# Start of a decoder step: the order of the first loads, dummy products, mixed chunks, and row factors spread without diagonals

## The reference, cut to what matters

```python
def rmsnorm(x, g):
    y = xf * lax.rsqrt(jnp.mean(xf * xf, -1, keepdims=True) + EPS)
    return (y * g).astype(x.dtype)

u = rmsnorm(x, norm_mix) @ w_in        # x: 520 x 1024, w_in: 1024 x 1216
cq, ckv, kr, up = u[..., :384], u[..., 384:640], u[..., 640:704], u[..., 704:]
c = rmsnorm(ckv, kv_norm)
...                                    # attention, pooling, memory attention, SwiGLU, final norm
```

## Time and profile before

| | us |
|---|---|
| median of 3 runs | 798.16 |
| lowest and highest | 796.25, 798.38 |
| span of the profiled execution | 797.1 |
| TensorE busy | 760.2 |
| DVE busy | 593.8 |
| ACT busy | 395.1 |
| GpSimd busy | 125.3 |

### The profile page before, as it was taken

The page is one execution under the profiler, slowest core; times in us unless marked ns, Lnnn a source line. Parts: engine busy times, 40 slices in busy tenths (PEclk is TensorE's granted clock), DMA queues, the critical chain, the costliest instruction groups (busy, mean ns, idle before and its releaser), DMA issues. The chain is left out here.

```text
span 797.1 us, 16215 instructions
## 1 busy us (share of the span) xinstructions
PE 760.2 (95%) x6264; PEld 727.7 (91%) x6264; DVE 593.8 (75%) x1170; ACT 395.1 (50%) x850; POOL 125.3 (16%) x179
## 2 busy tenths in 40 slices
PE   6999998897999997899999999999999999999996
PEld 6999887874899997888899999999999999999996
DVE  5778674687467699666478899888888869876664
ACT  5523776422265333665344356555555558433344
POOL 0376303230004731000046000000000000000000
PEclk9999999999999999999999999999999999999999
DMA  9423333462597558895243214333333333334303
GB/s 269 114 54 87 102 107 145 146 214 104 169 307 239 180 171 254 276 360 175 79 122 107 74 42 122 109 103 104 104 102 105 106 90 108 111 106 121 103 16 108
DMA packets 141777, 109.96 MB, mean 138 GB/s; under 512 B 9733, under 2 KB 133726, under 8 KB 138621
## 3 DMA queue, kind: packets, MB, share of 16 engines
q1 hardware_dynamic: 134830, 90.65, 37.5%
q0 software_dynamic: 3104, 14.68, 5.6%
q10 hardware_dynamic: 3767, 3.59, 1.3%
HBM read 103.93 MB, written 5.20 MB: 137 GB/s over the span
## 5 line engine op out<-in xcount | busy, mean ns | idle before, releaser
L1968 DVE TENSOR_TENSOR wlo<-wraw,whi 128x512 fp32r<-128x512 f32 (+1 forms) x178 | 129.8, 765 | 44.5 <-ACT whi L1271 34.7
L2906 PE MATMUL ps<-B_hi,whi 128*128 128x260 f32 x384 | 110.6, 288 | 2.4 <-DVE B_lo L1969 1.2
L2908 PE MATMUL ps<-B_hi,wlo 128*128 128x260 f32 x384 | 108.9, 284 | 0.0
L2907 PE MATMUL ps<-B_lo,whi 128*128 128x260 f32 x384 | 108.9, 283 | 0.0
L1271 ACT ACTIVATE whi<-wraw 128x512 fp32r<-128x512 f32 (+1 forms) x138 | 78.6, 616 | 53.9 <-DMA wraw<-in_w_mv_dram 10.7
L2906 PE MATMUL ps<-A_hi,whi 128*128 128x260 f32 x264 | 76.6, 290 | 0.3 <-ACT kn_lo L1365 0.3
L2906 PEld LDWEIGHTS ps<-B_hi,whi 128*128 128x128 f32 x384 | 72.8, 190 | 3.3 <-issue 1.5
L2907 PE MATMUL ps<-A_lo,whi 128*128 128x260 f32 x264 | 75.2, 285 | 0.0
L2908 PE MATMUL ps<-A_hi,wlo 128*128 128x260 f32 x264 | 75.1, 284 | 0.0
L2907 PEld LDWEIGHTS ps<-B_lo,whi 128*128 128x128 f32 x384 | 72.9, 190 | 0.0
L2908 PEld LDWEIGHTS ps<-B_hi,wlo 128*128 128x128 f32 x384 | 72.8, 190 | 0.0
(11 more groups left out here) (560 smaller groups left out, 2388.9 us busy)
## 6 DMA issues: line engine op xcount, KB each, us to landing
kv_slot<-in_cache_mem_k_dram SPq DMA_DIRECT2D x8, 1024.0 KB, 8.9
kv_slot<-in_cache_mem_v_dram SPq DMA_DIRECT2D x8, 1024.0 KB, 8.1
wraw<-in_w_out_dram SPq DMA_DIRECT2D x14, 512.0 KB, 4.3
wraw<-in_w_up_dram SPq DMA_DIRECT2D x12, 512.0 KB, 4.4
xraw<-in_w_gate_dram SPq DMA_DIRECT2D x20, 256.0 KB, 3.6
xraw<-in_w_up_dram SPq DMA_DIRECT2D x10, 512.0 KB, 4.1
wraw<-in_w_in_dram SPq DMA_DIRECT2D x9, 512.0 KB, 4.2
wraw<-in_w_gate_dram SPq DMA_DIRECT2D x18, 256.0 KB, 4.3
```

The lines of the kernel that those rows point to most:

```text
L1968: return dve.tensor_tensor(dst, src, high.bitcast(F32), ALU.subtract)
L2906: pe.matmul(dst, left[0], right[0], start=first, stop=False)
L2907: pe.matmul(dst, left[0], right[1], start=False, stop=False)
L2908: return pe.matmul(dst, left[1], right[0], start=False, stop=last)
```

## The change

- SyncE: tile 0 of w_in is issued ahead of x, and x comes in four quarters (256 columns, a semaphore each), then tile 1.
- TensorE: one dummy product (all-ones matrices, 512 columns, f32, into `accO`) before the identity is awaited, two more after the samples are turned.
- TensorE: chunks 0 and 1 are turned when the first quarter is in, 2 and 3 with the second, and so on. Chunks 0 and 1 of tile 0, turn 4 and 5, chunks 2 and 3 of tile 0, turn 6 and 7, chunks 0 to 3 of tile 1, then chunks 4 to 7 of both tiles in turn.
- ACT and DVE: both parts of an even chunk are read from PSUM; DVE's copy comes after its low part. ACT's copy and high part of odd chunks are as before. The samples' square comes first on ACT, ahead of the split of tile 0; row 1 is squared by DVE instead of ACT; the split of tile 2 is moved ahead of the last step of the row factors on both engines.
- Row factors, at both places: no diagonals; TensorE takes a column of factors, repeated 128 times, as loaded operand and the identity as the other.

```diff
-    o += [("in", 0, f) for f in (0, 1)] + [("xt", 6), ("xt", 7), ("bc",)] + [("in", 1, f) for f in (0, 1)]
+    o += [("in", 0, f) for f in (0, 1)] + [("xt", 6), ("xt", 7)] + [("in", 1, f) for f in (0, 1)] + [("bc",)]
...
-            for i in (0, 1):
-                half = slice(i * 512, (i + 1) * 512)
-                sp.dma_start(x_nat[:, 0:4, half], a["x_prompt"][0].rearrange("(t p) d -> p t d", p=P)[:, :, half]).then_inc(x_in[i], 16)
-                load_w(i)
+            load_w(0)
+            for i in range(4):
+                part = slice(i * 256, (i + 1) * 256)
+                sp.dma_start(x_nat[:, 0:4, part], a["x_prompt"][0].rearrange("(t p) d -> p t d", p=P)[:, :, part]).then_inc(x_in[i], 16)
+            load_w(1)
...
+            act.wait_ge(xs_in, 16)
+            act.activation(x_sq[0:NB, 3, :], x_nat[0:NB, 4, :], ACT.Square, accum_out=n1[0:NB, 4:5]).then_inc(x_squared, 1)
+            split_w(0)
             for c in range(KD):
...
-                    after(("x1", c))
-                    high(("x1", c), B_hi[:, c, 0:TP], xT[:, c, 0:TP], gain(G_MIX + c))
-                if c == 0:
-                    split_w(0)
+                    high(("x1", c), B_hi[:, c, 0:TP], full(act, ("xt", c)), gain(G_MIX + c))
                 if c == 3:
                     split_w(1)
+                if c == 5:
                     row_square(0)
-                if c == 5:
-                    row_square(1)
             row_square(3)
...
+            split_w(2)
             after(("ms", "n1"))
...
+                src = xT[:, c, 0:TP] if c % 2 else full(dve, ("xt", c))
+                low(("x1", c), B_lo[:, c, 0:TP], src, B_hi[:, c, 0:TP], gain(G_MIX + c))
...
             split_w(0)
+            for c in range(KD):
+                low_x(c)
+                if c % 2 == 0:
+                    copy_x(c)
+                if c == 3:
+                    split_w(1)
...
+            row_square(1, x_sq[:, 1, :])
+            row_square(2, x_sq2[:, :])
...
+            split_w(2)
             dve.wait_ge(root, ROOTS.index("n1") + 1)
-            step(dve.reciprocal(n1, n1))
-            for t in range(4):
-                dve.tensor_scalar(n1_diag[:, t, :], ident[:, :], n1[:, t:t + 1], None, ALU.mult)
-            value(("n1d",), dve.tensor_scalar(n1_diag_s[0:NB, :], ident[0:NB, 0:NB], n1[0:NB, 4:5], None, ALU.mult))
+            value(("n1d",), dve.reciprocal(n1, n1))
...
+            def run_up(n):
+
+                for _ in range(n):
+                    pe.matmul(accO, ones[:, :], ones[:, :].unsqueeze(1).to_broadcast([P, 4, P]), start=True, stop=True)
+
+            pe.wait_ge(ones_set, 1)
+            run_up(1)
             pe.wait_ge(ident_in, 16)
...
+            run_up(2)
+            for i in (0, 1):
+                pe.wait_ge(x_in[i], 16)
+                for c in (2 * i, 2 * i + 1):
+                    filled(turn_into(c), ("xt", c))
...
             in_chunk(0, 0)
-            pe.wait_ge(x_in[1], 16)
+            in_chunk(0, 1)
+            pe.wait_ge(x_in[2], 16)
             filled(turn_into(4), ("xt", 4))
             turn_into(5).then_inc(xt5_full, 1)
-            in_chunk(0, 1)
+            in_chunk(0, 2)
+            in_chunk(0, 3)
+            pe.wait_ge(x_in[3], 16)
             turn_chunk(6)
             turn_chunk(7)
+            in_bank.append([out(("in", 1, f)) for f in (0, 1)])
+            weights(S_IN + 1)
+            for k in range(4):
+                in_chunk(1, k)
+            for k in range(4, KD):
+                in_chunk(0, k)
+                in_chunk(1, k)
             b_bc = out(("bc",))
...
-                pe.matmul(b_bc[:, t * P:(t + 1) * P], ones[:, :], n1_diag[:, t, :], start=True, stop=True)
+                pe.matmul(b_bc[:, t * P:(t + 1) * P], n1[:, t:t + 1].to_broadcast([P, P]), ident[:, :], start=True, stop=True)
```

More of the change, by code:

```diff
@@ L449, in build @@
         qls = keep("qls", [2, NB, NH])
-        n1_diag = at("n1_diag", [4, P], F32, o_tmp)
-        n1_diag_s = at("n1_diag_s", [NB], F32, o_tmp + 2048)
         stat = keep("stat", [4, 4])
@@ L679, in build @@
         ident_in, xs_in, x_squared, n1_set = sem("ident_in"), sem("xs_in"), sem("x_squared"), sem("n1_set")
-        x_in = [sem(f"x_in{i}") for i in (0, 1)]
+        x_in = [sem(f"x_in{i}") for i in range(4)]
         mix_in = sem("mix_in")
@@ L1321, in _ @@
                 else:
-                    after(("x1", c))
-                    high(("x1", c), B_hi[:, c, 0:TP], xT[:, c, 0:TP], gain(G_MIX + c))
-                if c == 0:
-                    split_w(0)
+                    high(("x1", c), B_hi[:, c, 0:TP], full(act, ("xt", c)), gain(G_MIX + c))
                 if c == 3:
                     split_w(1)
+                if c == 5:
                     row_square(0)
-                if c == 5:
-                    row_square(1)
             row_square(3)
-            act.wait_ge(xs_in, 16)
-            act.activation(x_sq[0:NB, 3, :], x_nat[0:NB, 4, :], ACT.Square, accum_out=n1[0:NB, 4:5]).then_inc(x_squared, 1)
+            split_w(2)
             after(("ms", "n1"))
@@ L1404, in _ @@
             for m in range(10):
-                split_w(S_IN + m + 2)
+                if m:
+                    split_w(S_IN + m + 2)
                 if m == 2:
@@ L2015, in low_x, with row_square @@
             def low_x(c):
-                low(("x1", c), B_lo[:, c, 0:TP], xT[:, c, 0:TP], B_hi[:, c, 0:TP], gain(G_MIX + c))
-            copy_x(0)
-            low_x(0)
-            split_w(0)
[L2021 to L2031, removed]
+                src = xT[:, c, 0:TP] if c % 2 else full(dve, ("xt", c))
+                low(("x1", c), B_lo[:, c, 0:TP], src, B_hi[:, c, 0:TP], gain(G_MIX + c))
+            def row_square(t, scratch):
+                dve.tensor_tensor_reduce(scratch, x_nat[:, t, :], x_nat[:, t, :], 1.0, 0.0, ALU.mult, ALU.add,
+                                         n1[:, t:t + 1]).then_inc(x_squared, 1)
+            split_w(0)
+            for c in range(KD):
[4 more added lines that the diff above has]
+                    split_w(1)
             dve.wait_ge(n1_set, 1)
-            for i in (0, 1):
+            for i in range(4):
                 dve.wait_ge(x_in[i], 16)
-            dve.tensor_tensor_reduce(x_sq2[:, :], x_nat[:, 2, :], x_nat[:, 2, :], 1.0, 0.0, ALU.mult, ALU.add,
-                                     n1[:, 2:3]).then_inc(x_squared, 1)
+            row_square(1, x_sq[:, 1, :])
+            row_square(2, x_sq2[:, :])
             dve.wait_ge(x_squared, 5)
             value(("ms", "n1"), dve.tensor_scalar(n1, n1, 1.0 / D, EPS, ALU.mult, ALU.add))
+            split_w(2)
             dve.wait_ge(root, ROOTS.index("n1") + 1)
-            step(dve.reciprocal(n1, n1))
-            for t in range(4):
-                dve.tensor_scalar(n1_diag[:, t, :], ident[:, :], n1[:, t:t + 1], None, ALU.mult)
-            value(("n1d",), dve.tensor_scalar(n1_diag_s[0:NB, :], ident[0:NB, 0:NB], n1[0:NB, 4:5], None, ALU.mult))
+            value(("n1d",), dve.reciprocal(n1, n1))
             def rope(x, dst, rot_key, f, out_key):
@@ L2107, in _ @@
                     dve.wait_ge(root, ROOTS.index("nkv") + 1)
[L2108 to L2112, removed]
+                    value(("nkd",), dve.reciprocal(n1, n1))
                 if m == 6:
@@ L2937, in turn_into @@
                 return ins
-            pe.wait_ge(x_in[0], 16)
-            for c in range(4):
-                filled(turn_into(c), ("xt", c))
+            run_up(2)
[3 more added lines that the diff above has]
+                    filled(turn_into(c), ("xt", c))
             def turn_chunk(c):
@@ L2958, in _ @@
             in_chunk(0, 0)
-            pe.wait_ge(x_in[1], 16)
+            in_chunk(0, 1)
+            pe.wait_ge(x_in[2], 16)
             filled(turn_into(4), ("xt", 4))
             turn_into(5).then_inc(xt5_full, 1)
-            in_chunk(0, 1)
+            in_chunk(0, 2)
+            in_chunk(0, 3)
+            pe.wait_ge(x_in[3], 16)
             turn_chunk(6)
             turn_chunk(7)
-            b_bc = out(("bc",))
[L2966 to L2974, removed]
+            in_bank.append([out(("in", 1, f)) for f in (0, 1)])
[5 more added lines that the diff above has]
+                in_chunk(1, k)
+            b_bc = out(("bc",))
             after(("n1d",))
@@ L2977, in _ @@
             for t in range(4):
-                pe.matmul(b_bc[:, t * P:(t + 1) * P], ones[:, :], n1_diag[:, t, :], start=True, stop=True)
-            filled(pe.matmul(accO[:, 0:NB], ones[0:NB, :], n1_diag_s[0:NB, :], start=True, stop=True), ("bc",))
+                pe.matmul(b_bc[:, t * P:(t + 1) * P], n1[:, t:t + 1].to_broadcast([P, P]), ident[:, :], start=True, stop=True)
+            filled(pe.matmul(accO[:, 0:NB], n1[0:NB, 4:5].to_broadcast([NB, P]), ident[0:NB, 0:NB], start=True, stop=True), ("bc",))
             pe.wait_ge(consts_in, 32)
@@ L3015, in _ @@
                     for t in range(4):
```

(4 more changed lines are left out.)

## The result

Over 22 runs of each kernel the changed one takes 801.36 us (median; 796.74 to 805.11), the one before 798.16. The ratio is 1.0044, with a 95% interval of 1.0032 to 1.0056: slower by 0.3 to 0.6%. The prediction said 795.7 with a range of 794.3 to 798.2, so both the size and the sign are wrong. A few single runs, here and in the experiments, took far longer (841 to 4,189 us); the medians include them, the ratios leave them out. The profiled execution has a span of 800.4, 3.3 above that of before.

The account below looks back on a forecast made before the run. TensorE (busy 760.2 of 797.1 us) was taken as the bound, its late, partly half-rate start setting 27.07. Spreading at 24.7 saves 2.4, carried through: 798.16 - 2.4, rounded down to 795.7 us; range 794.3 to 798.2.

Parts of the forecast that it names:

- L: Start-up: moment when tile 1 of w_in lands, predicted at 14.1 us, bounds 13.4 and 15.5.
- the two known sizes: Start-up loads: per-packet and per-byte costs from 512 KB in 1,024 packets (1.85 us) and 256 (1.35) price an x quarter at 1.5.
- Repeating the column as loaded operand: Row-factor spreading: taken as no change in cost; bounds 0 and +1.05 us if each of eight instructions doubled.
- The gain of 2.4: Start of the row-factor spreading: moves from 27.07 to 24.7 us, 2.4 us less.
- the last one of the sum: After the start-up: later loads wait on the same chain's semaphores, so all 2.4 us carry through to the end.
- Rival 4: Later in the kernel: another wait takes the 2.4 us up, 797.2 to 798.2; chance 0.13, shared with a slow repeated-column load.
- Rival 3: Start-up: clock doesn't stay up; 1.7 us lost (797.5) or 7.0 (802.8); chance 0.13, of which 0.05 slower.
- so they are ready 1.4 us ahead of TensorE: Before the first spreading, kernel before: DVE's diagonals, written 24.39 to 25.66, taken to have 1.4 us slack.
- the fast level of turning and first products: Start-up: dummy products' claimed worth, turning x and first products at the 2.4 GHz level, products 0.12 us apart.

Follow-up runs that it names:

- experiment 4: Changed kernel with x loaded in two halves instead of four quarters; 797.18 us, ratio 0.9991 to the kernel before.
- experiment 1: Changed kernel with the eight page-table loads spread behind weight tiles 6 to 13, pooling copy and GpSimd's use of the ids later; 795.86 us, ratio 0.9975.
- experiment 3: Kernel before, with three more small, unused page-table loads ahead of the pooling-cache copy; 807.1 us, ratio 1.0109.
- experiment 11: Changed kernel run once more, unaltered, on another chip, against the kernel before; 802.39 us, ratio 1.0042.
- experiment 8: Changed kernel with three dummy products ahead of the last head's transposes of w_uk, where TensorE waits; 800.57 us, ratio 1.0023.
- experiment 6: Kernel of experiment 1 with DVE's diagonals back for the first spreading of row factors; 799.64 us, ratio 1.0019 to the kernel before.
- experiment 7: Kernel before with only the page-table loads spread as in experiment 1; 798.12 us, ratio 1.0003.
- experiment 5: Kernel of experiment 1 without its three dummy products; 795.12 us, ratio 0.9965 to the kernel before.
- experiment 10: Changed kernel with page-table loads spread, tile 2 evicted ahead of tile 4's low part, and no dummy products; 796.71 us, ratio 0.998.
- experiment 2: Changed kernel with DVE evicting tile 2 before making the low part of weight tile 4; 796.12 us, ratio 0.9973.

## Why the prediction was wrong

**Right.** Tile 1 is there at 14.06 (L = 14.1 was predicted), ACT idles 1.78 us ahead of it, the spreading begins at 24.99 (24.7) and tile 2 at 26.28 (26.0). A quarter of x costs what the two known sizes gave; the agreement to 0.04 us is partly luck, as the landing of tile 1 moves by 0.9 us between executions. Repeating the column as loaded operand costs nothing: 1.05 us for eight, as before. The gain of 2.4 was 2.08 at that place.

**The step that failed** is the last one of the sum: "Later loads wait on semaphores of this same chain, so I carry all of it through". That is true of the issue of tile 4's load, which came 2.5 us earlier (24.47 against 26.96). It isn't true of its landing, which came 2.3 us later. Ahead of it in SyncE's queue stand nine transfers that wait for no semaphore of their own, and they came 1.83 us later; with x in halves (experiment 4) they came as early as before, so it is the quarters that pushed them. The rows ahead of the prediction show that queue up to 3.30 us only, and I priced none of it behind. Experiment 1 shows that these transfers are what holds tile 4, and experiment 3 that more small loads in their row are enough by themselves.

**The rival that came.** Rival 4 said that another wait would take the gain up. It is the right kind, with two faults: I looked for it behind 80 us, since TensorE had no wait before, and I let it give back at most what was won. A wait that is just being avoided can come out longer than what was won, once the producer gets later and the consumer earlier. Here TensorE comes 2.08 us earlier, and DVE's eviction 1.72 us later (36.54 against 34.82: the load is 2.3 later, but DVE's low part ahead of the eviction took 1.8 us before and takes 1.2 now). Of these 3.8 us some 0.4 had been slack (35.23 to 35.6), and TensorE stood idle for 3.31.

**What was left out altogether** is the clock as a price of a wait. Rival 3 treats it at the start alone, where it stayed up. It fell inside the 3.31 us of idle time (granted 1.00 from 34 to 36 us, 0.52 from 36 to 38), and transposes and products at half rate until 42.96 cost 2.8 us, nearly as much as the wait. The Trainium skill's page TensorE: Matmul & The Clock Gate (Part 1, the section on oscillation) warns that waits for transfers in the middle of a kernel bring the lower clock back. The trace agrees: after 3.31 (changed), 3.96 (experiment 3) and 3.23 us (experiment 11) the products are slow, after 0.33 (experiment 4) and 0.94 (experiment 8, dummies ahead) they aren't.

**Mis-sized terms.** "so they are ready 1.4 us ahead of TensorE", of the diagonals, was read off the start of DVE's next work, at 25.66. The 8x8 diagonal starts at 25.54 and takes 1.23, so it ended at 26.77 and the slack was 0.3; experiment 6 shows TensorE waiting for exactly this end. From the end of the reciprocal to that of the last diagonal it is 2.46 us there (24.76 to 27.22), not 1.27. It makes the removal worth more than I gave it: with the diagonals the spreading began at 27.32, later than the 27.07 of before. The dummies, whose worth I put at the fast level of turning and first products, are worth 0.1 to 0.6 us in the traces.

**Open.** Two ratios are higher than the start of their traces shows: experiment 3 by 1.9 us, experiment 6 by 1.7. For experiment 6 the trace says where: against the kernel before it is 0.3 us late up to 113 us, 0.9 ahead at 200 us and 1.4 late from 377 us on. The same stretch moves other kernels whose code doesn't differ there: experiment 7 from 1.0 ahead to 0.2 late, experiment 8 from 0.6 to 3.4 late. The granted clock dips there in every profile but that of experiment 4 (1.00 from 200 to 350 us, against 0.98 before and 0.95 in experiment 8), which may be a part of it; I have no run that tells.

## What to carry to other kernels

When a start-up is shortened, follow each queue to the first load whose data someone waits for afterwards, and list what stands ahead of it; transfers that hang on nothing don't move up with the rest. An engine that is "never idle" may be met just in time: look at how long ahead of need each bank or buffer comes free, since that slack is all that an edit may use up. And price a wait of a few microseconds on TensorE twice, once for itself and once for the slow products behind it.

The version to keep is that of experiment 5 (page-table loads spread, no dummies), 0.9965; that of experiment 1 can't be told from it, and with the eviction ahead as well (experiment 10) it gave 0.998. One line of order on DVE (experiment 2) does as well.

## What the hardware showed

**Small loads hold up large ones.** DMA of the changed kernel from 23 to 29 us, packets by size:

```profile
23.00:29.00 6.00, 6.00 (x51) 5.86 (x50) 3.79 (x10) 1.36 (x3) 3.71 (x7) 1.00 0.05 1
```

```profile
DMA packets 696, 0.00 MB, mean 1 GB/s; under 512 B 696, under 2 KB 696, under 8 KB 696
```

Six microseconds, 696 packets, 1 GB/s, at a DMA share of 0.05, while 512 KB of weights, issued at 24.47, stand behind them. In the same six microseconds of experiment 1 it is 1055 packets and 0.54 MB. The Trainium skill's page DMA: Bandwidth & Descriptors (Rules for kernel authors) says that a load whose last dimension isn't contiguous becomes one descriptor per element; the trace agrees, as far as eight loads of 128 numbers in 4 KB can give that many packets. At 696 in 6 us, 1,024 of them take some 9 us (an estimate from this row); the trickle goes on past these rows, with 209 such packets from 29 to 31 us, and the weights come behind it. Why they go so slowly was not measured.

**An 8x8 instruction can cost 1.22 us.** It is 1.23 before and 1.22 in experiment 6 for a DVE product on 8x8 numbers, where four on 128x128 take 1.23 and 1.29 together. Before, DVE's next instruction started at 25.66 all the same, so what it costs is the time until its result can be used. In both traces GpSimd clears an area of 128x1296 over the same time: 25.52 to 26.74 beside 25.54 to 26.77 (before), 25.99 to 27.20 beside 26.00 to 27.22 (experiment 6). That the one makes the other slow was not tried.
